# The 16 gate columns of the first projection as full-precision products on four column groups of the array

## The reference, cut to what matters

```python
h = rms_norm(x, norm1_g[0])                  # y * g, y = x / rms(x)
p = h @ w_in                                 # (512, 1024) @ (1024, 3856)
...
qkv, b_in, a_in, z = split_cols(p_gdn, GDN_SIZES)   # b_in, a_in: 8 columns each
beta = jax.nn.sigmoid(b_in)
g = -jnp.exp(a_log) * jax.nn.softplus(a_in + dt_bias)
```

## Time and profile before

| | us |
|---|---|
| median of 3 runs | 1431.77 (1431.59 to 1433.36) |
| the profiled execution | 1431.76 |
| its span in the profile | 1430.0 |
| outside the span | 1.8 |
| TensorE busy | 1398.2 (98%) |
| ScalarE, VectorE, GpSimd busy | 599.0, 668.6, 525.9 |
| TensorE's mean granted clock | 0.999 of 2.4 GHz |

### The profile page before, as it was taken

One profiled execution on the slowest core, in us unless ns is written; L12 is line 12 of the kernel. 1 busy time (PEld: TensorE's weight loads), 2 busy tenths in 40 slices (PEclk: granted clock), 3 DMA queues, 4 the chain that ended last, 5 costly groups with the idle time before them and its releaser, 6 DMA issues.

```text
span 1430.0 us, 24988 instructions
## 1 busy us (share of the span) xinstructions
PE 1398.2 (98%) x10495; PEld 1149.3 (80%) x10495; DVE 668.6 (47%) x1112; ACT 599.0 (42%) x866; POOL 525.9 (37%) x239
## 2 busy tenths in 40 slices
PE   7999999999999999999999999999999999999998
PEld 5787778889878888888889977775688888888887
DVE  4665767788753314123144358936543223132231
ACT  5524763445545313232234465568635223131331
POOL 3544332111133443444345224332333443444341
PEclk9999999999999999999999999999999999999999
DMA  5332300000133233223224122210033223223221
GB/s 151 89 102 77 83 19 3 4 4 3 62 99 107 89 95 102 99 88 110 95 89 119 30 89 89 88 60 1 1 101 106 88 88 108 98 88 111 95 89 59
DMA packets 128977, 110.13 MB, mean 77 GB/s; under 512 B 10742, under 2 KB 126576, under 8 KB 128880
## 3 DMA queue, kind: packets, MB, share of 16 engines
q1 hardware_dynamic: 128000, 107.12, 23.9%
q10 hardware_dynamic: 880, 1.59, 0.3%
HBM read 106.60 MB, written 2.10 MB: 76 GB/s over the span
## 4 chain that ended last, share of the span: by engine, by line
PE 91%; DVE 3%; ACT 2%; POOL 2%; issue 1%; DMA 1%; SPq 0%; ACTq 0%; DVEq 0%; POOLq 0%
PE ps L569 22%; PE ps L571 22%; PE ps L570 22%; PE ps L713 5%; PE ps L1147 2%; PE ps L1157 1%; PE ps L576 1%; PE ps L577 1%; PE ps L581 1%; PE ps L1168 1%; PE ps L721 1%; PE ps L613 1%; PE ps L1122 1%; POOL pw_lo L2388 1%; PE ps L944 1%
## 5 line engine op out<-in xcount | busy, mean ns | idle before, releaser
L2475 POOL TENSOR_TENSOR w_lo<-lower,w_hi 128x2048 fp32r<-128x2048 f32 x83 | 385.2, 4641 | 524.0 <-ACT w_hi L1239 509.2
L569 PE MATMUL ps<-h_hi,w_lo 128*128 128x512 f32 x656 | 257.1, 392 | 0.4 <-POOL w_lo L2475 0.3
L570 PE MATMUL ps<-h_hi,w_hi 128*128 128x512 f32 x656 | 255.3, 389 | 0.0
L571 PE MATMUL ps<-h_lo,w_hi 128*128 128x512 f32 x656 | 255.3, 389 | 0.0
L1239 ACT ACTIVATE w_hi<-lower 128x2048 fp32r<-128x2048 f32 x83 | 158.4, 1909 | 226.3 <-PE ps L571 226.2
L569 PE MATMUL ps<-a_hi,w_lo 128*128 128x512 f32 x480 | 186.7, 389 | 0.0
L570 PE MATMUL ps<-a_hi,w_hi 128*128 128x512 f32 x480 | 186.7, 389 | 0.0
L571 PE MATMUL ps<-a_lo,w_hi 128*128 128x512 f32 x480 | 186.7, 389 | 0.0
L2180 DVE TENSOR_TENSOR lower<-lower,ps 128x512 f32<-128x512 f32 x60 | 41.2, 687 | 261.3 <-PE ps L571 240.3
L569 PEld LDWEIGHTS ps<-h_hi,w_lo 128*128 128x128 f32 x656 | 123.1, 188 | 28.8 <-issue 2.5
L570 PEld LDWEIGHTS ps<-h_hi,w_hi 128*128 128x128 f32 x656 | 123.2, 188 | 26.0 <-issue 0.7
(11 more groups left out here) (416 smaller groups left out, 2198.9 us busy)
## 6 DMA issues: line engine op xcount, KB each, us to landing
lower<-in_mlp_w_dram SPq DMA_DIRECT2D x64, 1024.0 KB, 5.2
lower<-in_ev_w_in_dram SPq DMA_DIRECT2D x30, 512.0 KB, 3.8
lower<-in_od_w_in_dram SPq DMA_DIRECT2D x10, 1024.0 KB, 5.1
lower<-in_ev_w_out_dram SPq DMA_DIRECT2D x4, 1024.0 KB, 5.9
lower<-in_od_w_out_dram SPq DMA_DIRECT2D x4, 1024.0 KB, 4.9
lower<-in_od_w_in_dram SPq DMA_DIRECT2D x6, 256.0 KB, 3.8
out_dram<-lower SPq DMA_DIRECT2D x6, 256.0 KB, 2.5
upper<-in_x_dram SPq DMA_DIRECT2D x1, 1024.0 KB, 7.1
```

Source lines behind the costliest of these rows:

```text
L569: pe.matmul(o, wl, xh, start=(i_ == 0), stop=False)
L570: pe.matmul(o, wh, xh, start=False, stop=False)
L571: mm = pe.matmul(o, wh, xl, start=False, stop=(i_ == n_ - 1))
L2475: pool.tensor_tensor(w_low(u)[:, :, 0:w], RAW[:, u % 2, :, 0:w], as_f32(w_high(u)[:, :, 0:w]), ALU.subtract)\
```

## The change

- The 16 raw gate columns are no longer split. POOL multiplies them by the norm's gain (`PC`, a column per slice of the input) into `WAB`, plain fp32, 32 columns wide for each of the 8 slices, of which the last 16 are zero. `WAB` lies where the third slot of `PWH` is.
- `gate_tile()` takes the place of tile(2) on PE: 8 fp32 matmuls of 32 columns against `XT`. Slices 0, 2, 4, 6 go to the four groups of 32 columns of the array, which write partitions 0, 32, 64 and 96 on of one bank, and slices 1, 3, 5, 7 are added in the same places. The bank then holds four partial sums.
- DVE scales all 128 rows of the bank by `RS`, in one instruction as before.
- The turn to tokens becomes a matmul of `ABF` (128 rows) with `FOLD`, a matrix made of four identities of 16, so that turning also adds the four partial sums. POOL builds `FOLD` by three additions.
- `tile_hi(2)` on ACT and `tile_lo(2)` on POOL are gone. The count `pw_lo` = 3 is now given by the product for `WAB`; `pw_hi` counts one less from tile 3 on.

```diff
+        WAB = flat(PW_HI + 2 * KT * P, KT * 32).rearrange("p (k n) -> p k n", k=KT)
+        FOLD = RSTD
...
+            def gate_tile():
+
+                o = bank_of(tile_q[2])
+                pe.wait_ge(pw_lo, 3)
+                for r in range(2):
+                    for g in range(4):
+                        mm = pe.matmul(o[32 * g:32 * g + 32, :], WAB[:, 2 * g + r, :], XT[:, 2 * g + r, :],
+                                       start=(r == 0), stop=(r == 1))
+                mm.then_inc(p_filled, 1)
...
-            tile(2)
+            gate_tile()
             tile(3)
...
-                mm = pe.transpose(o[:, 16 * i:16 * i + 16], ABF[0:16, i * P:(i + 1) * P], IDENT[0:16, 0:16])
+                mm = pe.matmul(o[:, 16 * i:16 * i + 16], ABF[:, i * P:(i + 1) * P], FOLD, start=True, stop=True)
...
-            tile_hi(2)
...
-            read0(dve.tensor_tensor(ABF[0:16, :], filled0(q)[0:16, :], RS[0][0:16, :], mul), q)
+            read0(dve.tensor_tensor(ABF, filled0(q), RS[0], mul), q)
...
-                pool.wait_ge(pw_hi, u + 1)
+                pool.wait_ge(pw_hi, u + 1 if u < 2 else u)
...
-            for u in range(3):
+            for u in range(2):
                 tile_lo(u)
+            t.link(pool.tensor_tensor(FOLD, IDENT[:, 0:16], IDENT[:, 32:48], ALU.add))
+            t.link(pool.tensor_tensor(FOLD, FOLD, IDENT[:, 64:80], ALU.add))
+            t.step(pool.tensor_tensor(FOLD, FOLD, IDENT[:, 96:112], ALU.add))
+            t.step(pool.memset(WAB[:, :, 16:32], 0.0))
+            pool.wait_ge(pr_full[0], 32)
+            pool.wait_ge(p_read[0], p_reads(pq["par0"]))
+            t.settle()
+            pool.tensor_tensor(WAB[:, :, 0:16], PRAW[:, 0, :, 0:16],
+                               PC[:, 0:KT].unsqueeze(2).broadcast_to([P, KT, 16]), mul).then_inc(pw_lo, 1)
```

## The result

The changed kernel takes 1435.77 us (median of 12 runs, 1434.46 to 1436.27), the kernel before 1431.65 beside it (12 runs): a ratio of 1.0027 with a 95% interval of 1.0019 to 1.0036. It is 4.1 us slower, where 1433.5 and "no change" had been forecast; the time lies above the range. A second set of eleven runs of each gave 1435.50 against 1432.20, ratio 1.0024 (1.0015 to 1.0033), so 3.3 to 4.1 us.

The account below looks back on a forecast made before the run. TensorE, busy 98% of the span, was taken as the bound. Tile 3's start 0, clock +1.5, turn +0.56 and slack -0.30 gave +1.76 us on 1431.76, so 1433.5; range 1431.0 to 1435.2.

Parts of the forecast that it names:

- The gate products: Gate tile on TensorE: 8 fp32 products replace 24 matmuls of 5.5 us and take 1.8 us (range 1.8 to 7.3).
- Nothing is gained by it: Ahead of tile 3: the shorter gate tile saves nothing directly, since tile 3 waits for POOL, ACT and the norm.
- the forecast's first rival: TensorE's gap ahead of tile 3: no fall of the clock, +0.26 us, 1432.0; chance 0.27.
- Tile 3 starts "at 32.40 as before: 0": Start of tile 3 on TensorE: unmoved at 32.40 us, since taking tile_hi(2) off idle ACT doesn't help; term 0.
- a moved chain to tile 3: Sign of a wrong prediction: the chain of waits leading to tile 3 moves at all.
- The clock: TensorE idles 4.3 us ahead of tile 3, its clock falls to half and costs 1.5 us (0 to 3.4).
- rival 2: Tile 3: clock stays low for a second stretch, over 5.2 us of half clock; +3.7 us, 1435.4; chance 0.12.
- The price of 1.35: Low clock stretch at 217.6 us in the kernel before: 2.7 us of matmuls at half speed lose 1.35 us.
- The turn: Turning gate rows to tokens on TensorE: fp32 matmuls take 0.91 us for 0.35, adding 0.56 (0 to 0.56).
- The slack: At L652 TensorE waited 0.3 us for ACT's Sigmoids, which takes 0.30 us off its lateness.
- rival 3: Gate tile: column groups don't run side by side, it takes 7.3 us, tile 3 starts 1.2 late; 1433.2; chance 0.04.
- Rival 4: Tile 3's start moves with the gate tile's end: 3.7 us less, 0.56 more, 1428.6; chance 0.03.

Follow-up runs that it names:

- run 3: Changed kernel without ACT's last token_sq wait and with four unused matmuls between gate tile and tile 3: 1431.97 us against 1432.19 for the kernel before.
- run 1: Changed kernel without ACT's last token_sq wait, so the table load of Ln comes early: 1435.00 us against 1432.19 for the kernel before.
- run 4: Kernel before with tile_hi(2) moved ahead of the last token_sq wait, so the table load comes late: 1433.24 us against 1432.19 unedited.
- run 6: Changed kernel with ACT's tile_hi(3) moved ahead of the norm's Ln: 1428.41 us against 1432.20 for the kernel before, ratio 0.9973.
- run 2: Changed kernel with five unused matmuls filling TensorE's gap between gate tile and tile 3: 1433.72 us against 1432.19 for the kernel before.
- run 5: Kernel before with its four transposes of the gate rows made fp32 matmuls against the identity: 1431.84 us against 1432.20 unedited.

## Why the prediction was wrong, step by step

**The gate products: right.** 1.8 us had been taken from rows that showed only two groups side by side; the trace has 1.86 from the first record of L605 to what follows it (26.16 to 28.02 in run 3). Four groups of 32 columns with all 128 rows run side by side at full factor, 7.3 / 1.86 = 3.9. By the figure of 2.38 that the Trainium skill (TensorE: Matmul & The Clock Gate, Part 3) gives for three groups, the estimate was 3.1 us; the measured four groups are faster.

**"Nothing is gained by it": right.** Tile 3 stood behind POOL, ACT and the norm, and run 3 shows that with both side costs taken away the change is worth zero (-0.2 us, with an interval from -1.6 to +1.0), in line with the +0.26 of the forecast's first rival.

**Tile 3 starts "at 32.40 as before: 0": wrong, by 1.26 us.** This is a step that failed, not a size. The prediction argued that taking `tile_hi(2)` off ACT can't matter, because ACT idled ahead of Ln. It looked at the time that the instruction took and not at what it did for the order: it took one of the two waits ahead of Ln, and without it the late one lands on the table load. The idle time of 3.80 us was the cover of that load of 1.28 us, and the prediction named no cover for it. Runs 1 and 4 show the mechanism from both sides. The prediction had named a moved chain to tile 3 as a sign that it is wrong, and that is what the trace shows.

**The clock: the mechanism right, its size too small.** A fall in the gap had been forecast at 1.5 us, with bounds of 0 and 3.4; the first profile had 2.61, the second 1.37. The length was read from the one low stretch of the kernel before, 3.4 us, as if it were a property of the fall; it can be twice that, which was rival 2's mechanism at a chance of 0.12, and 20 of 23 executions look like that. Its sign, over 5.2 us of half clock behind tile 3's start, is met with 5.7. It is not a consequence of the late table load: in run 1, with a gap of 4.15 us, close to the 4.3 of the prediction, the low stretch was 6.8 us as well. The price of 1.35 that the prediction gave the stretch at 217.6 was wrong too; the traces show 0.5 to 0.8 for it (run 3). TensorE also waits for other engines there, which may hide the rest; that is argued.

**The turn: 0.56 forecast, 0.46 measured, in the range.** Eight records with 16 moving columns take 0.81 us. **The slack: 0.30 forecast, 0.37 measured.** The wait at L652 is gone, as said.

**The two errors together.** With the table load's 1.26 alone the forecast sum would be +3.02 (1434.8), with the clock's 2.61 alone +2.87 (1434.6). Both lie inside the range; it took both to leave it. Rival 2's time of 1435.4 is near the measured one by coincidence: it had a clock term of 3.4 and no late table load.

**Rivals.** The groups do run side by side, so rival 3 was wrong. Rival 4, the gain coming through, was not what this kernel did, but it was the right picture of what stood in its way: run 6 moves ACT's high part of tile 3 to 23.07 and gets 3.8 us (3.69 in the trace up to L664). The sum of forecast terms was +1.76; with the measured ones it is 1.26 + 2.61 + 0.46 - 0.37 = 3.96, and 1431.76 + 3.96 = 1435.7. The median is 1435.77; the profiled execution took 1435.24, for the reasons under the table.

## What to carry to other kernels

Making a stage shorter on the busiest engine, just ahead of a wait that did not move, turns busy time into idle time, and here TensorE's clock was low when the work resumed, so that the kernel became slower than with the gap filled by useless work (run 1 against run 3): look at what releases the next instruction before counting the saving, and move that first. An instruction that is taken away from an idle engine is not free either if waits stand on both sides of it; compare the order with its waits, above all where a table load follows. Profiled executions of one kernel differ in things that the change doesn't touch (here the start of the norm's sums, and the low stretch near 220 us): compare distances between marks, and look at more than one execution's clock. Where an engine waits for a result that it doesn't need (tile 3's high part behind the norm), the instructions that need nothing can go ahead into the idle time.

## What the runs showed of the hardware

- A low stretch of TensorE's clock was 3.4 or 6.8 us long, in two profiles of the same program with the same gap of 5.49 us. Its start is not tied to the gap's start: it came 4.3 us into the gap in the first profile of the changed kernel, 5.1 us in the second, and 1.4 us after the work had resumed behind a gap of 2.24 us. A gap of 3.10 us was seen without a fall, and so were 1.75 and 1.01. The low stretch near 220 us in the trace of before is missing in the profiles of runs 2, 3 and 6. How a gap's place decides was not settled by these runs.
- At the start of the program the fp32 transposes of 128 columns began 0.21 us apart, and 0.11 us apart from 11.2 us on in one profile and from 12.8 in another. The rows of the granted clock read 1.00 on both sides of the change of pace.
- fp32 products of 32 columns on four column groups, with four different moving operands, took 1.86 us for eight of 512 tokens, where one full-width product takes 0.92.
- An fp32 matmul with 128 weight columns and 16 moving ones costs 0.20 us with weights of 128 rows (0.81 / 4) and 0.25 with weights of 16 rows (0.99 / 4, run 5). The transposes took 0.09 each (0.35 / 4).
- A table load took 1.28 us, and the Ln behind it started 0.01 us after its end.
